# The last down products by token halves, and two half feature tiles first in the next stage

## The reference

```
x = x + 0.5 * rms_norm(swiglu(rms_norm(x, g[0]), ffn_wgu[i, 0], ffn_wd[i, 0]), g[1])
h = rms_norm(x, g[2])          # then the mixer's first product h @ w_in
rms_norm(x, g) = x * rsqrt(mean(x * x) + eps) * g
```

## Time and profile before

| what | value |
|---|---|
| median of 3 runs | 3579.15 us (3578.71 to 3584.44) |
| the profiled execution's own time | 3584.59 us |
| its span, first to last instruction | 3582.5 us |
| PE busy | 3496.0 us (98% of the span), 18831 matmuls |
| DVE, ACT, POOL busy | 1954.6, 1247.9, 439.1 us |
| mean granted TensorE clock | 0.990 |

### The profile page before, as it was taken

How to read it: one execution, slowest core, us unless ns; L and a number is a source line. 1 busy time by engine, 2 the same in 40 slices (tenths; PEclk the granted TensorE clock), 3 DMA queues, 4 the chain that set the end, 5 groups by cost and what they waited for, 6 DMA issues and landing times.

```text
span 3582.5 us, 47270 instructions
## 1 busy us (share of the span) xinstructions
PE 3496.0 (98%) x18831; PEld 2790.0 (78%) x18831; DVE 1954.6 (55%) x2698; ACT 1247.9 (35%) x1776; POOL 439.1 (12%) x351
## 2 busy tenths in 40 slices
PE   8999999999999999999998999999999999999998
PEld 6888888645888878887777788878888777778887
DVE  5655563365555565446567554556445534465455
ACT  5632232465422242224644332233223423242222
POOL 1220011010100021112023010111111000011111
PEclk9999999899999999999999999999999999999999
DMA  3332234100322323232200133223232222213231
GB/s 119 106 110 94 94 94 94 36 1 24 94 94 94 97 92 99 89 106 89 63 22 15 49 109 101 91 86 100 89 105 94 83 83 83 83 60 105 94 104 61
DMA packets 232555, 295.94 MB, mean 83 GB/s; under 512 B 21893, under 2 KB 201464, under 8 KB 232392
## 3 DMA queue, kind: packets, MB, share of 16 engines
q1 hardware_dynamic: 230864, 290.48, 25.5%
q0 software_dynamic: 1152, 3.05, 0.4%
q10 hardware_dynamic: 376, 0.12, 0.0%
HBM read 291.53 MB, written 2.10 MB: 82 GB/s over the span
## 4 chain that ended last, share of the span: by engine, by line
PE 90%; DVE 5%; ACT 3%; issue 1%; DMA 0%; SPq 0%; DVEq 0%; ACTq 0%
PE bank L309 26%; PE bank L311 25%; PE bank L310 25%; PE bank L338 1%; PE bank L340 1%; PE bank L339 1%; PE bank L2986 1%; DVE wlo L305 1%; PE bank L1500 1%; PE bank L1569 1%; PE bank L2453 1%; PE bank L1585 1%; ACT whi L299 1%; ACT fsum L1666 1%; PE bank L1599 0%
## 5 line engine op out<-in xcount | busy, mean ns | idle before, releaser
L309 PE MATMUL bank<-h_hi,whi 128*128 128x512 f32 x2748 | 1083.0, 394 | 21.8 <-DVE h_lo L789 9.9
L310 PE MATMUL bank<-h_lo,whi 128*128 128x512 f32 x2748 | 1069.3, 389 | 0.0
L311 PE MATMUL bank<-h_hi,wlo 128*128 128x512 f32 x2748 | 1069.3, 389 | 0.0
L299 ACT ACTIVATE whi<-raw 128x2048 fp32r<-128x2048 f32 x266 | 508.6, 1912 | 1245.0 <-PE bank L311 1192.6
L305 DVE TENSOR_TENSOR wlo<-raw,whi 128x2048 fp32r<-128x2048 f32 x266 | 613.0, 2305 | 323.6 <-ACT whi L299 323.5
L309 PEld LDWEIGHTS bank<-h_hi,whi 128*128 128x128 f32 x2748 | 517.3, 188 | 147.2 <-issue 32.6
L311 PEld LDWEIGHTS bank<-h_hi,wlo 128*128 128x128 f32 x2748 | 517.2, 188 | 107.7
L310 PEld LDWEIGHTS bank<-h_lo,whi 128*128 128x128 f32 x2748 | 517.3, 188 | 107.5 <-issue 3.6
L309 PE MATMUL bank<-u_hi,whi 128*128 128x512 f32 x1440 | 561.6, 390 | 4.6 <-DVE arena L3062 2.4
L311 PE MATMUL bank<-u_hi,wlo 128*128 128x512 f32 x1440 | 560.3, 389 | 0.0
L310 PE MATMUL bank<-u_lo,whi 128*128 128x512 f32 x1440 | 560.3, 389 | 0.0
(11 more groups left out here) (442 smaller groups left out, 3116.6 us busy)
## 6 DMA issues: line engine op xcount, KB each, us to landing
raw<-in_ffn_wgu SPq DMA_DIRECT2D x88, 1024.0 KB, 5.1
raw<-in_ffn_wd SPq DMA_DIRECT2D x44, 1024.0 KB, 4.9
raw<-in_mlp_w_up SPq DMA_DIRECT2D x32, 1024.0 KB, 5.7
raw<-in_mlp_w_down SPq DMA_DIRECT2D x32, 1024.0 KB, 4.9
raw<-in_odd_w_in SPq DMA_DIRECT2D x24, 1024.0 KB, 5.1
raw<-in_even_w_in SPq DMA_DIRECT2D x13, 1024.0 KB, 5.3
raw<-in_rg_w_in SPq DMA_DIRECT2D x8, 1024.0 KB, 5.5
raw<-in_odd_w_out SPq DMA_DIRECT2D x8, 1024.0 KB, 5.1
```

Of the source, the lines that this page charges most:

```text
L299: e.activation(whi[:, n % 2, :], raw[:, n % 2, :], ACT.Copy).then_inc(hi_ready, 1)
L309: pe.matmul(o, w_hi, r_hi, start=first, stop=False)
L310: pe.matmul(o, w_hi, r_lo, start=False, stop=False)
L311: return pe.matmul(o, w_lo, r_hi, start=False, stop=last)
```

## The change

In the four feed-forward stages f1, s00, s01 and s10, each followed by a norm that it owes, the last down chunk makes tiles 0 to 3 whole, then tiles 4 to 7 for the LEFT tokens, then tile 4 RIGHT, then the LEFT sum over the features, then tiles 5 to 7 RIGHT, then the RIGHT sum. A sum is now three products instead of four: POOL adds the squares of tiles 0 to 3 whole and those of tiles 4 and 5 in halves onto the same sum. The squares have a place of their own each, but that of tile 7 takes tile 3's place. DVE adds, ACT squares and both roots are placed between the new pieces in a written-out order. The first two feature tiles of the next stage, k = 0 and 1, are both made by halves, and `pe_first` takes (c, k) = (0,0), (1,0), (0,1), (1,1) LEFT, the same four RIGHT, then (0,2), (0,3), (1,2) and on. The filling products are left out there. The stages after a mixer and the last one stay as they were.

```diff
--- before.py
+++ after.py
...
@@ -266,6 +268,10 @@
                 k += FFN[step[1]]["groups"]
         norm_no = {i: sum(s_[0] == "norm" for s_ in PLAN[:i]) for i in range(len(PLAN))}
         owed_no = {i: sum(s_[0] in ("norm", "post") and s_[1] is not None for s_ in PLAN[:i]) for i in range(len(PLAN))}
+
+        def halves(stage):
+            return PLAN[stage][0] == "norm" and PLAN[stage][1] is not None and PLAN[stage - 1][0] == "ffn"
+        halves_no = {i: sum(halves(s_) for s_ in range(1, i)) for i in range(len(PLAN))}
         swi_base = {n_: b_ - sum(FFN[m_]["groups"] for m_ in FFN if not FFN[m_]["swiglu"]) for n_, b_ in ffn_base.items()}
 
...
@@ -411,7 +417,33 @@
                 def free(m):
                     if m > 3:
                         pe.wait_ge(added, at(8 * (b + g) + m + 5, i, 16))
+                if i is None and g == f["groups"] - 1 and halves(stage + 1):
+                    down_halves(n, half, 2 * (g % 2), free)
+                    return
                 pe_chunk(pe, n, 2, 8, u_hi, u_lo, lambda m: pbank[half + m % 4][:, :], free, i, dn, k0=2 * (g % 2))
+
+            def down_halves(n, half, k0, free):
+                pe.wait_ge(lo_ready, n + 1)
+
+                def tile(m, cut):
+                    for k in range(2):
+                        c = k * KT * P + m * P
+                        ins = three(pe, pbank[half + m % 4][:, cut], whi[:, n % 2, c:c + P], wlo[:, n % 2, c:c + P],
+                                    u_hi[:, k0 + k, cut], u_lo[:, k0 + k, cut], k == 0, k == 1)
+                    return ins
+                for m in range(4):
+                    tile(m, slice(0, S)).then_inc(tiles_out, 1)
+                for m in range(4, 8):
+                    free(m)
+                    tile(m, LEFT).then_inc(half_out, 1)
+                for m in range(4, 8):
+                    if m == 7:
+                        pe.wait_ge(tail_a, owed_no[stage + 1] + 1)
+                    else:
+                        pe.wait_ge(half_added, 3 * halves_no[stage + 1] + m - 3)
+                    tile(m, RIGHT).then_inc(tiles_out, 1)
+                    if m == 4:
+                        pe_half_sum(pe, stage + 1, LEFT)
...
@@ -460,6 +492,15 @@
             def down(g, n, i, dn, dt):
                 pass
             ffn_walk(e, name, gu, down)
+
+        def late_right(e, stage, m):
+            name = PLAN[stage][1]
+            f, g = FFN[name], FFN[name]["groups"] - 1
+            n = where[name] + f["gu"] * (g + 1) + g
+            e.wait_ge(tiles_out, before[n] + m + 1)
+            e.wait_ge(added, 8 * (ffn_base[name] + g) + m + 1)
+            e.tensor_tensor(f["dst"][:, m, RIGHT], f["dst"][:, m, RIGHT], pbank[4 * (g % 2) + m - 4][:, RIGHT], ALU.add)\
+                .then_inc(added, 1)
 
         def dve_ffn(e, name, stage):
...
@@ -501,7 +542,8 @@
             def down(g, n, i, dn, dt):
                 final = i is None and g == f["groups"] - 1
                 half = 4 * (g % 2)
-                for m in range(8):
+                by_halves = final and halves(stage + 1)
+                for m in range(4 if by_halves else 8):
                     if m == 4 and not final:
                         dve_lo(e, n + 1, i, dn, dt)
                     e.wait_ge(tiles_out, at(before[n] + m + 1, i, dt))
@@ -519,6 +561,15 @@
                         lo_tile(e, stage + 1, m - 2)
                     if final and not early_lo(stage) and m == 1:
                         dve_lo(e, n + 1)
+                if by_halves:
+                    hj = halves_no[stage + 1]
+                    for m in range(4, 8):
+                        e.wait_ge(half_out, 4 * hj + m - 3)
+                        e.wait_ge(added, 8 * (b + g) + m + 1)
+                        e.tensor_tensor(dst[:, m, LEFT], dst[:, m, LEFT], pbank[half + m - 4][:, LEFT], ALU.add)\
+                            .then_inc(tail_a if m == 7 else half_added, 1)
+                    late_right(e, stage, 4)
+                    late_right(e, stage, 5)
                 if not final and (i is not None or g < f["groups"] - 2 or early_lo(stage)):
                     dve_lo(e, n + 2, i, dn, dt)
...
@@ -559,6 +610,8 @@
 
         def owed_bank(stage, part):
             swiglu = PLAN[stage - 1][0] == "ffn" and FFN[PLAN[stage - 1][1]]["swiglu"]
+            if halves(stage) and not swiglu and part == RIGHT:
+                return pbank[4][:, part]
             return pbank[(5 if swiglu else 3) - (part == RIGHT)][:, part]
 
...
+
+        def act_root(e, stage, chain, i, part):
+            e.wait_ge(f_sum, 2 * owed_no[stage] + i + 1)
+            chain(e.activation(rstd[:, part], owed_bank(stage, part), ACT.Ln, bias=eps[:, 0:1], scale=1.0 / D))
+            e.activation(rstd[:, part], rstd[:, part], ACT.Exp, scale=-0.5).then_inc(f_root, 1)
+
+        def act_halves(e, stage, chain):
+            src = x if PLAN[stage][1][0] == "x" else fsum
+            j, hj = owed_no[stage], halves_no[stage]
+            sec, g0 = PLAN[stage][2:4]
+
+            def right(k):
+                final(e, stage, k)
+                e.activation(tmp[:, 3 if k == 7 else k, RIGHT], src[:, k, RIGHT], ACT.Square).then_inc(f_sq, 1)
+
+            def high(k, part, signal):
+                e.activation(h_hi[:, k, part], x[:, k, part], ACT.Copy, scale=gain(sec, g0 + k)).then_inc(signal, 1)
+            for k in range(4):
+                final(e, stage, k)
+                e.activation(tmp[:, k, :], src[:, k, :], ACT.Square).then_inc(f_sq, 1)
+            for k in range(4, 7):
+                e.wait_ge(half_added, 3 * hj + k - 3)
+                e.activation(tmp[:, k, LEFT], src[:, k, LEFT], ACT.Square).then_inc(half_sq, 1)
+            e.wait_ge(f_add, 4 * j + 3)
+            e.wait_ge(tail_a, j + 1)
+            e.activation(tmp[:, 3, LEFT], src[:, 7, LEFT], ACT.Square).then_inc(f_sqa, 1)
+            right(4)
+            right(5)
+            act_root(e, stage, chain, 0, LEFT)
+            right(6)
+            e.wait_ge(x_new_a, j + 1)
+            high(0, LEFT, n_hi_a)
+            right(7)
+            act_hi_piece(e, stage, 0)
+            e.wait_ge(x_new_b, hj + 1)
+            high(1, LEFT, n_hi_b)
+            act_root(e, stage, chain, 1, RIGHT)
+            for k in range(KT):
+                e.wait_ge(x_new, KT * j + k + 1)
+                if k < 2:
+                    high(k, RIGHT, n_hi)
+                else:
+                    act_high_tile(e, stage, k)
+                if k in (2, 4, 6):
+                    act_hi_piece(e, stage, k // 2)
+                e.activation(fsum[:, k, :], x[:, k, :], ACT.Square).then_inc(n_sq, 1)
 
...
@@ -608,7 +707,9 @@
         def act_norm(e, stage, chain):
             j = norm_no[stage]
             kind = PLAN[stage - 1][0]
-            if PLAN[stage][1] is not None:
+            if halves(stage):
+                act_halves(e, stage, chain)
+            elif PLAN[stage][1] is not None:
                 act_owed(e, stage, chain)
...
@@ -680,6 +781,25 @@
 
         def pool_owed(e, stage):
             j = owed_no[stage]
+            if halves(stage):
+                hj = halves_no[stage]
+                for k in range(1, 4):
+                    e.wait_ge(f_sq, KT * j + k + 1)
+                    if k > 1:
+                        e.wait_ge(f_add, 4 * j + k - 1)
+                    e.tensor_tensor(acc, tmp[:, 0, :] if k == 1 else acc, tmp[:, k, :], ALU.add).then_inc(f_add, 1)
+                e.wait_ge(f_add, 4 * j + 3)
+                e.wait_ge(half_sq, 3 * hj + 1)
+                e.tensor_tensor(acc[:, LEFT], acc[:, LEFT], tmp[:, 4, LEFT], ALU.add).then_inc(half_sum, 1)
+                e.wait_ge(half_sq, 3 * hj + 2)
+                e.wait_ge(half_sum, 3 * hj + 1)
+                e.tensor_tensor(acc[:, LEFT], acc[:, LEFT], tmp[:, 5, LEFT], ALU.add).then_inc(half_sum, 1)
+                e.wait_ge(f_sq, KT * j + 5)
+                e.tensor_tensor(acc[:, RIGHT], acc[:, RIGHT], tmp[:, 4, RIGHT], ALU.add).then_inc(half_sum, 1)
+                e.wait_ge(f_sq, KT * j + 6)
+                e.wait_ge(half_sum, 3 * hj + 3)
...
@@ -706,7 +826,29 @@
                     e.wait_ge(n_add, 7 * j + k - 1)
                 e.tensor_tensor(acc, tmp[:, 4, :] if k == 1 else acc, tmp[:, 4 + k % 3, :], ALU.add).then_inc(n_add, 1)
 
+        def pe_half_sum(pe, stage, part):
+            j, hj = owed_no[stage], halves_no[stage]
+            out = owed_bank(stage, part)
+            if part == LEFT:
+                pe.wait_ge(half_sq, 3 * hj + 3)
+            else:
+                pe.wait_ge(f_sq, KT * j + 7)
+            pe.matmul(out, ones[:, :], tmp[:, 6, part], start=True, stop=False)
+            if part == LEFT:
+                pe.wait_ge(half_sum, 3 * hj + 2)
+            else:
+                pe.wait_ge(f_add, 4 * j + 4)
+            pe.matmul(out, ones[:, :], acc[:, part], start=False, stop=False)
+            if part == LEFT:
+                pe.wait_ge(f_sqa, j + 1)
+            else:
```

(96 more changed lines are left out.)

## The result

The changed kernel takes 3595.27 us (median of 5, 3591.81 to 3602.85) against 3579.15; the ratio is 1.0037, with the 95% interval 1.0026 to 1.0047, so 9 to 17 us slower, 13 in the middle. The two medians lie 16.1 apart, but five executions each are few: in the sessions of the experiments the median of the kernel before was 3581.3 to 3583.6. The forecast was 3589.0, in 3579 to 3598.

The account below looks back on a forecast made before the run. The prediction took one long dependent chain across engines, with PE almost idle under it, as what bounds these places. 0.8 after f1 + 3 x 2.4 elsewhere + 1.8 for the clock = +9.8 us, giving 3589.0, range 3579 to 3598.

Parts of the forecast that it names:

- The sum at tile 3: Delay of next-stage tile 3, counted from tile 4 of the last down chunk, over four places; forecast total +9.8 us.
- the walk: Instruction lists laid out with measured pitches from tile 4 to next-stage tile 3: +0.8 us after f1, +2.4 at three others.
- step 5: Without fillers, PE's idle stretch lets the clock fall at half to two thirds of the places: 0.45 us average, +1.8 total.
- Step 1: At the LEFT sum, PE waits for POOL's half adds until about +6.2; the last product starts at +6.75.
- Rival (a): At the LEFT sum, POOL holds nothing up; everything comes 2.25 us earlier, 3578, no change; chance 0.20 together with (d).
- Steps 2 and 3: ACT's LEFT root behind tile 5 RIGHT's square, scaling 1.15 late; RIGHT sum before next stage, first product +13.1 for +11.45.
- Step 4: RIGHT's root stands behind tile 1 LEFT's high part on ACT; RIGHT scaled at +14.8, 4.4 late; tile 3 at +22.95.
- Rival (b): The clock falls at all four places, nothing absorbed: 1.6 us each, 14.4 in all, 3593.5; chance 0.22.
- Rival (c): Faster: LEFT's root gets through under RIGHT's products; at most 22 us to gain, half gives 3568; chance 0.08.

Follow-up runs that it names:

- e1_fill: The changed kernel plus nine filling products ahead of the LEFT sum and nine ahead of the RIGHT sum, four places; ratio 1.0021 to the kernel before.
- e5: The changed kernel, POOL adding only squares of tiles 0 to 2, tile 7's square in tile 0's place, six PE products per half sum; ratio 1.0028 to before.
- e2_nofill: The kernel before, only without its six filling products in each of the four places; ratio 1.0012 to the kernel before.
- e6: The changed kernel, same pieces reordered: PE's RIGHT tiles before the LEFT sum, DVE's before the norm, ACT's before LEFT's root; no fillers; ratio 1.0 to before.
- e10: The changed kernel with the order of e6 and three fillers behind the RIGHT sum; ratio 1.0005 to the kernel before.
- e10_order_fill3: Full name of e10: new list order, three fillers behind the RIGHT sum; ratio 1.0005 to the kernel before.
- e11: The order of e6 with three fillers, but only feature tile 0 of the next stage by halves; ratio 1.0025 to the kernel before.

## Why the prediction was right, step by step

The path was the one forecast: POOL, then the orders of the lists, with the clock on top. The sum at tile 3 came out at 9.9 for 9.8, and e1_fill, where the clock holds, measures the part without it: 8.1 for 8.0. That both agree to 0.1 us is partly luck. After f1 the walk was 0.4 short (20.7 for 20.25, in the change and in e1_fill), at the three other places 0.1 long each; and the clock came out at its size with the wrong places (step 5).

- **Step 1, POOL.** Third add done at +4.4, second half add at +6.1 (1630.32 + 0.72; forecast +6.15), last product of the LEFT sum at +6.75 (+6.75). The half adds took 0.72 beside 0.74 assumed. Rival (a) falls: POOL did hold the sum, in all four places. But taking POOL out of the wait (e5) gave 1.1 us a place, not 2.25; the last product came 1.0 earlier, since the sum then has six products. The half adds of 0.72 ran with DVE idle; the prediction had DVE on PSUM beside them. The first whole add, beside the weights' low part on DVE, took 2.62 at 1623.87, the next two 2.71 together. That agrees with the Trainium skill (GPSIMD Engine Reference, Key points), by which GpSimd contends for its SBUF interfaces with DVE instructions that have two SBUF inputs.
- **Steps 2 and 3, the lists.** With the clock held (e1) the first product comes at +13.5 after s00 for +13.1 forecast, RIGHT at +16.85 for +16.95, tile 3 at +22.8 for +22.95. In the change itself the scaling of LEFT came at +10.85, one later than the +9.85 forecast, because tiles 5 to 7 RIGHT ran at the low clock. The walk did not have that, nor the 0.26 us that PE stands idle between the RIGHT sum and the first product, a wait for nothing that the profile shows. After f1 in e1_fill the first product comes at +13.5 for +12.65 and RIGHT at +16.4 for +15.5.
- **Step 4, RIGHT's root.** DVE scales RIGHT at +15.75 (1640.69) for +14.8, again one late for the same reason; tile 3 waits 0.86 for its low part, as forecast.
- **Step 5, the clock.** At tile 3 of the profiled execution the size was right (1.8 for 1.8), by luck, for the places were half wrong. I had it fall behind the idle time ahead of the RIGHT sum, at half to two thirds of the places. It fell at all four, at three of them behind the wait for POOL, 1.95 us long, so that it slowed products that LEFT's root waits for. By place, the change against e1_fill: 0, 1.0, -0.1 and 0.8 us at tile 3. Where it fell late, after s01, all went into waits; the 0 after f1 hides up to 0.4 of the fillers' own delay. Over all executions the clock's part is nearer 5 us, by the estimate at an equal clock; 1.8 was too small for that. Rival (b) had it cost 1.6 at every place; the places of the profile speak against it, while in the time its 14.4 in all lies inside 9 to 17, so the time alone doesn't rule it out. The Trainium skill (Perfetto Trace Analysis, Matmul Optimizations) wants matmuls back to back, and e1_fill and e2_nofill agree: 1.8 and 3.2 us at tile 3 hang on the fillers.
- **Rival (c).** Even with the best order tried the gain at tile 3 was 2 us of the 22 at hand. LEFT's logarithm is then at +7.4, and what is left is the chain root, scale, high, low for each half.
- **The measured time** lies above the forecast, 13 for 9.8, inside the interval. By the equal clock it splits into 8.2 for the orders, as forecast (8.0), and about 5 for the clock. In which stages those 5 arise the profiles don't show, since the clock falls at other moments in each execution and one was profiled.

The kernels e6 and e10 undo the loss and are like the kernel before; none beats it beyond its interval.

## What to carry to other kernels

When a piece of work is cut so that its first half can run ahead, look in each engine's list for what now stands ahead of that first half: here PE's LEFT sum stood ahead of RIGHT products, ACT's and DVE's RIGHT pieces ahead of LEFT's root, and a slow helper (POOL, two more adds in a row) at the head of all. The same pieces in another order made 10 us of difference at tile 3 with the clock held (8.1 in e1_fill, -2.0 in e10_order_fill3), and a single move in one list less than all together. In this kernel fillers were worth having where PE would idle, but only behind the last product that someone waits for.

## What was unexpected of the hardware

A PE busy for 1.45 us of 3.4, idle for 1.95 in one piece, was followed by 3.4 us at the 1.2 GHz level, and what such a stretch cost depended on what ran in it: nothing where the products had waits behind them anyway (after s01), 1.0 us where they lay ahead of a root (after s00). In e11 a stretch with 1.04 of 3.0 us busy was followed by 6.8 us at that level, although PE was busy for 5.5 of them. And over 196 executions a thousandth of the mean granted clock, 7.2 us at the lower level, was worth 2.1 us of span: less than a third of the stretch, where half would go if PE were the limit all along.
